# Scan of a two-block network: rows scaled head by head on ScalarE, and the middle convolution tap read by ScalarE from PSUM

## What is computed

```python
xbc = jax.nn.silu(depthwise_conv(xbc, w_ssm_conv[l], b_ssm_conv[l]))   # 7 taps a channel, 3072 channels
# ssd_scan, in chunks of 128 tokens, once forwards and once backwards:
xd = x * dt[..., None]
cb = jnp.einsum('bclgn,bcsgn->bcgls', Cc, Bc)
y_diag = jnp.einsum('bcgls,bcgjls,bcsgjp->bclgjp', cb, decay, xd)
states = jnp.einsum('bclgn,bcgjl,bclgjp->bcgjpn', Bc, decay_to_end, xd)
y_off = jnp.einsum('bclgn,bcgjpn,bcgjl->bclgjp', Cc, prev, jnp.exp(a_cs))
y = y_f + y_b + d_skip[:, None] * x
```

## Time before, and how to read its profile

| | us |
|---|---|
| median of 3 runs (2845.06 to 2850.16) | 2847.4 |
| the profiled execution | 2850.86 |
| its span in the profile | 2849.1 |
| TensorE busy / VectorE / ScalarE / GpSimd in the span | 2662.9 / 1036.7 / 643.9 / 205.1 |

### The profile page before, as it was taken

How to read it: one execution, slowest core, us unless ns; L and a number is a source line. 1 busy time by engine, 2 the same in 40 slices (tenths; PEclk the granted TensorE clock), 3 DMA queues, 4 the chain that set the end, 5 groups by cost and what they waited for, 6 DMA issues and landing times.

```text
span 2849.1 us, 39926 instructions
## 1 busy us (share of the span) xinstructions
PE 2662.9 (93%) x17315; PEld 1622.5 (57%) x17315; DVE 1036.7 (36%) x1502; ACT 643.9 (23%) x1146; POOL 205.1 (7%) x218
## 2 busy tenths in 40 slices
PE   8987899999979989898988997999999999999996
PEld 6754468888767767677767996333333333333332
DVE  4335444433245767577775334011111111111111
ACT  3344332222122314132226222100000000000001
POOL 0021000000001212021120000000000000000000
PEclk9998899999989999999999999999999999999998
DMA  5200022212213123140341234999999999999993
GB/s 197 89 0 1 26 93 94 114 63 100 108 39 121 52 86 102 40 132 25 97 137 59 90 130 183 387 397 396 399 397 395 401 404 401 394 397 396 394 400 140
DMA packets 92618, 560.77 MB, mean 197 GB/s; under 512 B 15236, under 2 KB 48004, under 8 KB 59812
## 3 DMA queue, kind: packets, MB, share of 16 engines
q1 hardware_dynamic: 40320, 514.89, 45.8%
q10 hardware_dynamic: 47236, 30.42, 3.9%
q0 software_dynamic: 4896, 12.98, 1.7%
HBM read 541.97 MB, written 16.29 MB: 196 GB/s over the span
## 4 chain that ended last, share of the span: by engine, by line
PE 86%; DVE 7%; ACT 4%; issue 2%; DMA 1%; POOL 0%; ACTq 0%; POOLq 0%; DVEq 0%; SPq 0%
PE PS L1027 35%; PE PS L497 17%; PE PS L929 4%; PE PS L707 4%; PE PS L703 4%; PE PS L704 4%; PE PS L934 2%; PE PS L678 2%; PE PS L560 1%; PE PS L561 1%; PE PS L564 1%; PE PS L510 1%; PE PS L1017 1%; DVE H L1786 1%; PE PS L846 1%
## 5 line engine op out<-in xcount | busy, mean ns | idle before, releaser
L497 PE MATMUL PS<-U,ring 128*128 128x264 f32 x2304 | 547.8, 399 | 18.7 <-DVE arena L1797 18.7
L497 PEld LDWEIGHTS PS<-U,ring 128*128 128x128 f32 x2304 | 450.8, 197 | 109.6 <-issue 30.5
L1027 PE MATMUL PS<-expert_ring_low,U 128*32 128x512 f32 x4608 | 509.7, 594 | 0.9 <-DVE U L2011 0.9
L1027 PE MATMUL PS<-expert_ring_high,U 128*32 128x512 f32 x4608 | 504.8, 592 | 0.0
L1027 PEld LDWEIGHTS PS<-expert_ring_high,U 128*32 128x32 f32 x4608 | 148.0, 110 | 336.9 <-issue 335.9
L1027 PEld LDWEIGHTS PS<-expert_ring_low,U 128*32 128x32 f32 x4608 | 146.2, 110 | 332.8 <-issue 331.7
L1786 DVE SCALAR_TENSOR_TENSOR H<-arena,par,H 128x528 f32<-128x528 f32 x240 | 189.3, 834 | 1.4
L2023 DVE TENSOR_TENSOR H<-H,PS 128x512 f32<-128x512 f32 x32 | 22.0, 688 | 439.7 <-PE PS L1027 424.2
L703 PE MATMUL PS<-UX,WF 128*128 128x512 f32 x352 | 137.9, 392 | 0.8 <-DVE UX L1545 0.8
L704 PE MATMUL PS<-UX,WF 128*128 128x512 f32 x352 | 137.0, 389 | 0.0
L1222 ACT ACTIVATE WF<-ring 128x1024 fp32r<-128x1024 f32 (+1 forms) x76 | 72.0, 948 | 245.6 <-PE PS L707 245.6
(11 more groups left out here) (326 smaller groups left out, 3192.8 us busy)
## 6 DMA issues: line engine op xcount, KB each, us to landing
expert_ring_low<-w_experts SPq DMA_DIRECT2D x96, 2048.0 KB, 11.6
expert_ring_high<-w_experts SPq DMA_DIRECT2D x96, 2048.0 KB, 11.5
ring<-w_gu SPq DMA_DIRECT2D x11, 2048.0 KB, 7.9
ring<-ssd_sums ACTq DMA_DIRECT2D x32, 512.0 KB, 8.0
ring<-w_xbc SPq DMA_DIRECT2D x8, 1536.0 KB, 6.6
ring<-w_down SPq DMA_DIRECT2D x8, 1408.0 KB, 6.0
ring<-w_in SPq DMA_DIRECT2D x5, 2048.0 KB, 7.9
ring<-w_conf SPq DMA_DIRECT2D x8, 1024.0 KB, 5.3
```

Source lines behind the costliest of these rows:

```text
L497: last = nc.tensor.matmul(PS[0:M, banks[i], 0:hi - lo], lhs(k), rhs(k)[:, lo:hi], start=(k == 0), stop=(k == K - 1))
L1027: mm = nc.tensor.matmul(PS[QUAD * t:QUAD * t + QUAD, bank, :], stat(t), move(t), start=start, stop=stop)
```

## The change

Three things are done together.

- GpSimd's 52 broadcast products in the scan are gone; it only masks. ScalarE does the same products head by head: eight ACTIVATE instructions of 64 columns for each, with Copy and a scale for each partition (`scaled`, called by `back_scaled`, `front_scaled`, `skip_scaled`), 416 in all.
- The middle one of the seven convolution taps is computed by ScalarE straight from PSUM into CO (`mid_tap`), once a tile. VectorE does the six side taps, all of which add to CO. What VectorE waited for before writing CO (the transpose of tile i-2), ScalarE now waits for.
- In a convolution tile ScalarE takes the transposed tile first, then does the middle tap, then the SiLU. At the start of the state loop the four DMA issues follow the last take of a transposed tile, then come the first two scalings, and the "late" gate (in group 3 alone) stands behind these; it stood ahead of the DMA issues.

```diff
--- before.py
+++ after.py
@@ -370,6 +370,11 @@
 
 
 
+        MID_TAP = SSM_TAPS // 2
+
+        def conv_row(g, t):
+            return 16 + (0 if t == 2 else 4) + g if t in (2, 5) else 4 * g + (t if t < 2 else t - 1)
+
         pieces = []
         for m in range(FFT):
             for part in range(2):
@@ -1265,7 +1270,20 @@
                 if i >= 2:
                     act.wait_ge(S("conv_done"), i - 1)
                 b = bank(("xb", g, t))
-                free(A(tok(XP[:, i % 2, 3:3 + T2], T2), PS[:, b:b + 2, 0:HT], ACT.Copy), ("xb", g, t))
+                A(tok(XP[:, i % 2, 3:3 + T2], T2), PS[:, b:b + 2, 0:HT], ACT.Copy)
+
+            def mid_tap(g, t):
+
+                i = 6 * g + t
+                b = bank(("xb", g, t))
+                if i >= 2:
+                    g2, t2 = divmod(i - 2, 6)
+                    if t2 in (2, 5):
+                        act.wait_ge(S("conv_ready"), i - 1)
+                    else:
+                        got(act, ("tr", g2, t2))
+                w = pcol("ssm_w", conv_row(g, t) * SSM_TAPS + MID_TAP)
+                free(A(tok(CO[:, i % 2, :], T2), PS[:, b:b + 2, 0:HT], ACT.Copy, scale=w), ("xb", g, t))
 
             def conf_gate(u):
                 got(act, ("cg", u))
...
@@ -1351,32 +1371,75 @@
                 link(A(dst[:, 0:4, :], PS[:, 4, :].rearrange("p (c n) -> p c n", c=4), ACT.Copy))
                 free(A(dst[0:META, 4, :], PS[0:META, 5, 0:P], ACT.Copy), tag)
 
+            def scaled(dst, g, c, by, sem):
+
+                n = CHUNKS[c][1]
+                for h in range(GH):
+                    ins = A(dst[0:n, h * HD:h * HD + HD], XS[0:n, c, h * HD:h * HD + HD], ACT.Copy, scale=by[0:n, h:h + 1])
+                ins.then_inc(S(sem), 1)
+
+            def back_scaled(g, s):
+
+                c = NC - 1 - s
+                if s >= 2:
+                    got(act, ("sb", g, c + 2))
+                elif g > 0:
+                    got(act, ("sf", g - 1, 3))
+                scaled(XW[:, s % 2, :], g, c, W2[:, c, 32 + GH * g:32 + GH * g + GH], "xwb_ready")
+
+            def front_scaled(g, c):
+
+                if c >= 2:
+                    got(act, ("sf", g, c - 2))
+                else:
+                    got(act, ("sb", g, 1))
+                scaled(XW[:, c % 2, :], g, c, W2[:, c, GH * g:GH * g + GH], "xwf_ready")
+
+            def skip_scaled(g, c):
+
+                i = NC * g + c
+                if i >= 1:
+                    act.wait_ge(*freed(("yd", (i - 1) // NC, (i - 1) % NC)))
+                scaled(XD, g, c, par[:, PARAMS["ssm_d"] + GH * g:PARAMS["ssm_d"] + GH * g + GH], "xd_ready")
+
             XS_AT = {0: 0, 1: 1, 3: 2, 4: 3}
             for g in range(GROUPS):
                 for t in range(6):
                     if g > 0 or t >= 2:
                         conv_tile(g, t)
+                    if t >= 3:
+                        take_turned(g, t - 3)
+                    if g > 0 or t >= 2:
+                        mid_tap(g, t)
                     if t >= 1:
                         conv_silu(g, t - 1)
-                    if t >= 3:
-                        take_turned(g, t - 3)
                 take_turned(g, 3)
                 gates_out((g, "conv"))
                 conv_silu(g, 5)
                 take_turned(g, 4)
-                gates_out((g, "late"))
                 fr_load(g, 0)
                 fr_load(g, 1)
+                if g == 0:
+                    act.wait_ge(S("w2_ready"), 1)
+                act.wait_ge(*freed(("tr", g, 4)))
+                back_scaled(g, 0)
+                back_scaled(g, 1)
+                gates_out((g, "late"))
                 for s in range(4):
                     tag = ("zt", 4 * g + s)
                     got(act, tag)
                     b = bank(tag)
                     free(A(tok(YT[:, 4 * g + s, :], T2), PS[:, b:b + 2, 0:HT], ACT.Silu), tag)
+                    if s < 2:
+                        back_scaled(g, s + 2)
                 decays(g, 0)
                 decays(g, 1)
                 for c, (t0, n) in enumerate(CHUNKS):
                     if c >= 2:
                         decays(g, c)
+                    if c < 4:
+                        front_scaled(g, c)
+                    skip_scaled(g, c)
                     gates_out((g, c))
                     if c % 2 == 1 and g < GROUPS - 1:
                         conf_gate(2 * g + CONF_AHEAD + c // 2)
@@ -1809,22 +1872,14 @@
                 for t in range(6):
                     i = 6 * g + t
                     dve.wait_ge(*freed(("xb", g, t)))
-                    j = 16 + (0 if t == 2 else 4) + g if t in (2, 5) else 4 * g + (t if t < 2 else t - 1)
-                    if i >= 2:
-                        g2, t2 = divmod(i - 2, 6)
-                        if t2 in (2, 5):
-                            dve.wait_ge(S("conv_ready"), i - 1)
-                        else:
-                            got(dve, ("tr", g2, t2))
-                    w0 = PARAMS["ssm_w"] + j * SSM_TAPS
+                    w0 = PARAMS["ssm_w"] + conv_row(g, t) * SSM_TAPS
                     co, xp = CO[:, i % 2, :], XP[:, i % 2, :]
-                    for k in range(SSM_TAPS):
-                        if k == 0:
-                            ins = V_.tensor_scalar(co, xp[:, 0:T2], par[:, w0:w0 + 1], None, MUL)
-                        else:
-                            dve.wait_ge(S("conv_tap"), (SSM_TAPS - 1) * i + k)
-                            ins = V_.scalar_tensor_tensor(co, xp[:, k:k + T2], par[:, w0 + k:w0 + k + 1], co, MUL, ADD)
-                        ins.then_inc(S("conv_tap" if k < SSM_TAPS - 1 else "conv_done"), 1)
+                    side_taps = [k for k in range(SSM_TAPS) if k != MID_TAP]
+                    for n, k in enumerate(side_taps):
+                        if n > 0:
+                            dve.wait_ge(S("conv_tap"), (len(side_taps) - 1) * i + n)
+                        V_.scalar_tensor_tensor(co, xp[:, k:k + T2], par[:, w0 + k:w0 + k + 1], co, MUL, ADD)\
+                            .then_inc(S("conv_tap" if n < len(side_taps) - 1 else "conv_done"), 1)
                         if k in (2, 5):
                             some_taps(1, 2 * g + 2)
 
@@ -2086,15 +2141,6 @@
             pool.wait_ge(S("h_summed"), DT)
             pool.dma_start(h_dram, H[:, :, :]).then_inc(S("h_saved"), 16)
 
-            def bc(ap, n, w):
-                return ap.unsqueeze(2).to_broadcast([n, GH, w])
-
-            def scaled(dst, g, c, n, by, sem):
-
-                G_.tensor_tensor(dst[0:n].rearrange("p (h w) -> p h w", h=GH),
-                                 XS[0:n, c, :].rearrange("p (h w) -> p h w", h=GH), bc(by, n, HD), MUL)\
-                    .then_inc(S(sem), 1)
-
             def masked(g, c):
 
                 i = NC * g + c
@@ -2105,34 +2151,9 @@
                     G_.affine_select(out=v, in_=v, compare_op=ALU.is_ge, fill=-BIG, base=0, pattern=[[0, GH], [sign, n]],
                                      channel_multiplier=-sign).then_inc(S("fr_masked"), 1)
 
-            pool.wait_ge(S("h_saved"), 16)
-            pool.wait_ge(S("w2_ready"), 1)
             for g in range(GROUPS):
-                h8 = slice(GH * g, GH * g + GH)
-                h8b = slice(32 + GH * g, 32 + GH * g + GH)
-                pool.wait_ge(*freed(("tr", g, 4)))
-                for s, c in enumerate(range(NC - 1, 0, -1)):
-                    n = CHUNKS[c][1]
-                    if s >= 2:
-                        got(pool, ("sb", g, c + 2))
-                    elif g > 0:
-                        got(pool, ("sf", g - 1, 3))
-                    scaled(XW[:, s % 2, :], g, c, n, W2[0:n, c, h8b], "xwb_ready")
-                    if s in (1, 2):
-                        masked(g, s - 1)
-                for c, (t0, n) in enumerate(CHUNKS):
-                    i = NC * g + c
-                    if i >= 1:
-                        pool.wait_ge(*freed(("yd", (i - 1) // NC, (i - 1) % NC)))
-                    scaled(XD, g, c, n, par[0:n, PARAMS["ssm_d"] + GH * g:PARAMS["ssm_d"] + GH * g + GH], "xd_ready")
-                    if c < 4:
-                        if c >= 2:
-                            got(pool, ("sf", g, c - 2))
-                        else:
-                            got(pool, ("sb", g, 1))
-                        scaled(XW[:, c % 2, :], g, c, n, W2[0:n, c, h8], "xwf_ready")
-                    if c + 2 < NC:
-                        masked(g, c + 2)
+                for c in range(NC):
+                    masked(g, c)
             got(pool, ("so", DT - 1))
             pool.wait_ge(S("h_saved"), 16)
             pool.dma_start(H[:, :, :], h_dram).then_inc(S("h_back"), 16)
```

More of the change, by code:

```diff
@@ L1289, in _ @@
             conv_tile(0, 0)
+            mid_tap(0, 0)
             conv_tile(0, 1)
+            mid_tap(0, 1)
             conf_gate(0)
@@ L1332, in conv_silu @@
                 act.wait_ge(S("conv_done"), i + 1)
```

(22 more changed lines are left out.)

## The result

The changed kernel takes 2865.45 us (median of 4 runs, 2864.64 to 2868.77) against 2846.46 in the same comparison (4 runs, 2845.06 to 2850.16): a ratio of 1.0065, 95% interval 1.005 to 1.008. It is slower by 19.0 us. The forecast was 2861.4, slower by 14.0. The profiled execution took 2866.2, with a span of 2864.1, so 15.3 more than the profiled one of before.

A forecast was written before the change was run, and what follows sets the result against it. TensorE and its waits were taken as the bound. Convolution tiles -13.1 with clock, state loop start +25.8, its clock +2.8, chunk loop -1.5 gave +14.0 us on 2847.4, so 2861.4 us, range 2848 to 2874.

The forecast's parts named there:

- What bounds the kernel: Scan: TensorE, busy 643.6 of 724 us, is the bound; moving other engines' work matters only where TensorE waits.
- Convolution tiles, waits: TensorE's 12 waits for the take, 29.5 us in all, shrink to 1.57 each: 10.7 us gained.
- The middle tap: Convolution tiles: VectorE's 12 us of saved taps buy nothing by themselves.
- Start of the state loop: Scalings wait behind four DMA issues on ScalarE, so TensorE's first product comes later: 25.8 us lost over four groups.
- The chunk loop: Added scalings stay hidden and a TensorE wait in group 3, chunk 1, goes: 1.5 us gained.
- The clock: TensorE's clock falls behind long waits: 2.4 us given back in convolution tiles, 2.8 lost at the state loop.
- Convolution tiles, -2.4: The slow projection behind group 0's long wait returns to full clock: 2.4 us gained, bounds 0 and about 6.
- State loop, +2.8: Longer waits at its start lower TensorE's clock: 0.35 us in groups 0 to 2, 1.7 in group 3.
- Rival A: State loop start: DMA issues don't hold the scalings back; 12.5 us faster, 2834.9 us; chance 0.10.
- Rival B: Scan: relief of VectorE shortens TensorE's waits for it; 8.7 us faster, 2838.7 us; chance 0.05.
- Rival C: Chunk loop: costlier scalings make ScalarE late for masks and first scaling; 10 us more, 2871.4 us; chance 0.17.

The follow-up runs named there:

- e1: Kernel before with only the convolution part of the change, products left on GpSimd: 2832.7 us, ratio 0.9947.
- e2: Kernel before with only the take of the transposed tile put ahead of the SiLU, seven taps on VectorE: 2831.5 us, ratio 0.9943.
- e6: Kernel before with only the take of a transposed tile one tile earlier in ScalarE's list: 2811.3 us, ratio 0.9877.
- e7: e6 with the middle tap on ScalarE, products still on GpSimd: 2811.9 us, ratio 0.9876 against the kernel before.
- e9: e4 with chunk 0's front scaling moved ahead of the second head set's 32 decays: 2835.7 us, ratio 0.9965 against the kernel before.
- e3: Kernel before with only the scalings moved to ScalarE, convolution tiles as before: 2876.9 us, ratio 1.0104.
- e4: Changed kernel with the four DMA issues placed behind the first two scalings: 2834.9 us, ratio 0.9958 against the kernel before.
- e8: e4 with the take of a transposed tile one tile earlier: 2814.7 us, ratio 0.9886 against the kernel before.
- e5: Changed kernel with two of the four DMA issues placed behind the first two scalings: 2841.0 us, ratio 0.9979 against the kernel before.

## Why the prediction came out as it did

The mechanism and the sign were right, and the total came out near in part by luck; the scan cost 3.6 us more than forecast.

- **What bounds the kernel.** TensorE's waits, and its clock behind them: of the scan's 17.6 us, 17.1 are idle time of TensorE. The share of busy time of the engines that were relieved said nothing.
- **Convolution tiles, waits.** Forecast 29.5 to 18.8, measured 18.9. The long wait of group 0 did become one of 1.58.
- **The middle tap.** Forecast to buy nothing: e1 and e2 agree, e6 and e7 agree.
- **Start of the state loop.** Forecast +25.8, measured +27.2, within its bounds (24.6 to 27.4). The issues took 6.49 us in group 1 (forecast 6.61) and 7.25 in group 3 (7.0), eight scalings 2.00 (1.95). Too small was the 0.15 us for all gaps: in group 1 the scaling began 0.10 after the issues' end, in group 3 0.39 (1382.10 + 7.25 against 1389.74), and TensorE some 0.27 after eight scalings in both. By group it was 7.2 in group 1, 15.4 in groups 0 and 2, 4.6 in group 3, against 7.1, 14.8 and 3.9.
- **The chunk loop.** Forecast -1.5, measured +0.2: this term failed. The gain that was named did come: the wait of 3.35 us in group 3, chunk 1, became 1.50. The mask stayed hidden, as forecast: in group 1 the issues ahead of it began 3.8 us later against the loop (forecast 3.9), and it ended 2.2 us later and 1.3 us ahead of the decays. The forecast's own figures were less consistent: a mask that ends at 1103.1 leaves nothing ahead of decays at 1103.12, not half a us. What I left out is that the new list has a wait of its own in group 3: I placed the two scalings "ahead of the gate's take and the DMA issues" and asked what they delay, not what stands ahead of them. The 32 decays of 9.45 us do. TensorE waits 2.07 us for the front scaling of chunk 0 behind them, more than the 1.5 that was to be gained. Moving the scaling ahead of half of them (e9) removes that wait, and one of 2.74 appears in chunk 2; no other order was tried.
- **The clock.** Forecast -2.4 + 2.8 = +0.4, measured +0.5 of busy time. That is right by errors that cancel, as luck would have it.
  - *Convolution tiles, -2.4.* I priced one slow projection. In before's trace the transposes and projections behind four of the twelve waits were slow, 8.0 us in all: 4.6 in group 0, behind the long wait and the next one, and 3.4 in group 2, behind two waits of 2.20. In the changed kernel none is (both views below). So the term was -8.0, beyond its far bound of about 6. But e3, which has the same waits as before, was slow only behind the long one, for 1.8 us: how much of the 8.0 another execution would show is open.
  - *State loop, +2.8.* The first product and the projection behind it took 46.0 us over the four groups in place of 42.3, so +3.7. By group that is 0.0, +1.2, -0.8 and +3.3, where 0.35 three times and 1.7 were forecast. That a wait of 10 us leaves the clock low at least as long as one of 3.5 did not hold in groups 0 and 2.
  - *The rest.* The other 4.8 us of busy time lie elsewhere in the scan, and no term stood for them. One row of it is the projection behind the wait for the front scaling, 9.00 us in place of 7.29.

Before, group 2, and the same place in the changed kernel (timeline of PE). The granted clock over the first transpose was 0.50, over the second pair 1.00:

```profile
1196.10 1.30 PE L816 MATMUL PS<-consts_sb,SQ 128*128 128x128 f32 x5 [2.20 <-ACT arena L1352]
1197.20 8.40 PE L497 MATMUL PS<-U,ring 128*128 128x264 f32 x32
```

```profile
1200.17 0.73 PE L821 MATMUL PS<-consts_sb,SQ 128*128 128x128 f32 x5 [1.58 <-ACT arena L1372]
1200.74 7.29 PE L502 MATMUL PS<-U,ring 128*128 128x264 f32 x32
```

- **Rival A**, that issues don't hold the scalings back, is refuted: the scaling began 6.60 us behind the take, not under 3, with 6.34 us of idle time put to the issues, and moving them is worth 30.6 us. e4, which brings this rival's condition about in another way, took 2834.9, the rival's own figure; that the digits agree is chance, since the convolution part alone gained 14.8 us (e1) and not the 13.1 in the rival's sum.
- **Rival B**, relief of VectorE reaching TensorE, is refuted: the 240 31-tap instructions took 180.5 us in place of 189.3, the waits for a conf bank are the same 18.7, and e1 with 24 taps fewer on VectorE is no faster than e2.
- **Rival C**, ScalarE late in the chunk loop, happened in one chunk and for another reason than the one it named: its price was 10 us, and the waits for a scaling in the chunk loop were 2.07 and 0.28.

## What to carry to other kernels

Before moving work to another engine, read what stands ahead of it in that engine's list, DMA issues included, and add their measured time to the wait of whoever is next; here four issues, unnoticed while GpSimd worked beside them, cost more than the change could gain. And where the engine that bounds the kernel waits for a PSUM bank to be emptied, ask first how early the emptying could run: placing the take one tile earlier was worth 36 us (e6), by order alone. That is the version to keep; neither the middle tap (e7) nor the scalings on ScalarE (e8) made it faster.

## What the runs showed of the hardware

- The four issues are unequal. In the changed kernel's trace the first takes 0.37 us in each group, the second 0.60 to 0.78, the third 2.5 to 3.4 and the fourth 2.4 to 2.9. Why was not tried.
- Issue and computation on ScalarE stand in order one way only. What is written behind an issue waits for it (6.34 us; in e5 1.01). But an issue written behind sixteen ACTIVATEs began when five had begun, at 1030.01 in e4, and the other eleven went on beside it. ScalarE's list is not worked off strictly in order there.
- The granted clock fell to 0.50 behind some waits of 2.20 us and not behind others: three of eleven in before's convolution tiles, none of eleven in e3's. Behind the twelve waits of 1.58 us in e1, in e2 and in the changed kernel it never did.
- Ending 29.5 us of short waits gave 36.2 us of the median (e6). In the profiled execution TensorE's busy time in the scan was 10.8 us less for the same work, and the granted clock of the scan 0.95 in place of 0.94.
